# Layer 1's state-space outputs for the latents only, and one expert of full width instead of two

## What is computed

```python
for direction in range(2):
    s_ctx = diag_scan(lam_bar, einsum('blgh,gph->blgp', ug_ctx, b_bar), None, reverse)
    s_end = s_ctx[:, 0] if reverse else s_ctx[:, -1]
    s_lat = diag_scan(lam_bar, einsum('blgh,gph->blgp', ug_lat, b_bar), s_end, reverse)
    y_lat = y_lat + einsum('blgp,ghp->blgh', s_lat, cmat).real
    if need_ctx:
        y_ctx = y_ctx + einsum('blgp,ghp->blgh', s_ctx, cmat).real
```

## Time and profile before

| | us |
|---|---|
| median of 3 runs | 1811.03 (1811.0 to 1811.67) |
| profiled execution, its own time | 1811.02 |
| its span | 1809.3 |
| TensorE matmul busy | 1719.1 |
| VectorE busy | 651.3 |
| ScalarE busy | 351.9 |
| TensorE weight load busy | 909.5 |

### The profile page before, as it was taken

The page is one execution under the profiler, slowest core; times in us unless marked ns, Lnnn a source line. Parts: engine busy times, 40 slices in busy tenths (PEclk is TensorE's granted clock), DMA queues, the critical chain, the costliest instruction groups (busy, mean ns, idle before and its releaser), DMA issues.

```text
span 1809.3 us, 22168 instructions
## 1 busy us (share of the span) xinstructions
PE 1719.1 (95%) x9128; PEld 909.5 (50%) x9128; DVE 651.3 (36%) x1476; ACT 351.9 (19%) x742; POOL 73.6 (4%) x147
## 2 busy tenths in 40 slices
PE   6999999799999999988988899999999999999996
PEld 3655454288888744436766753344344322222232
DVE  5988961755554305074895520000000000000002
ACT  4324550311110000035364320000000000000001
POOL 2110100000000210000110000000000000000000
PEclk9999999899999999999999899999999999999998
DMA  8414542713333332361433089999899999999992
GB/s 304 145 20 167 188 130 81 232 48 93 94 93 79 74 78 78 111 233 47 117 91 98 1 346 370 377 375 409 318 396 359 409 347 410 392 408 344 409 377 111
DMA packets 194980, 396.11 MB, mean 219 GB/s; under 512 B 34339, under 2 KB 104587, under 8 KB 188730
## 3 DMA queue, kind: packets, MB, share of 16 engines
q1 hardware_dynamic: 189504, 391.23, 60.2%
q0 software_dynamic: 4112, 3.34, 1.2%
q10 hardware_dynamic: 1258, 0.07, 0.0%
HBM read 389.36 MB, written 1.05 MB: 216 GB/s over the span
## 4 chain that ended last, share of the span: by engine, by line
PE 87%; DVE 8%; ACT 3%; DMA 1%; issue 1%; ACTq 0%; DVEq 0%
PE ps L946 85%; PE ps L949 2%; DMA ring<-in_w_in_dram 1%; DVE rstd L1768 1%; DVE aT L1961 1%; DVE hT L1790 0%; DVE aT L1776 0%; DVE work L1785 0%; DVE aT L1785 0%; ACT work L645 0%; ACT work L646 0%; DVE work L1677 0%; DVE work L1679 0%; DVE work L1682 0%; ACT work L757 0%
## 5 line engine op out<-in xcount | busy, mean ns | idle before, releaser
L946 PE MATMUL ps<-ring,work 128*64 128x512 f32 (+4 forms) x2656 | 553.4, 515 | 1.7 <-ACT work L890 1.1
L946 PEld LDWEIGHTS ps<-ring,work 128*64 128x64 f32 (+2 forms) x2656 | 188.7, 136 | 351.9 <-issue 348.4
L946 PE MATMUL ps<-aT,ring 128*128 128x256 f32 (+1 forms) x800 | 235.4, 443 | 5.3 <-ACT work L757 2.7
L946 PE MATMUL ps<-work,ring 128*128 128x512 f32 (+1 forms) x656 | 237.0, 514 | 1.3 <-DVE work L2077 1.3
L2215 DVE TENSOR_TENSOR work<-work,ps 128x512 f32<-128x512 f32 (+4 forms) x26 | 20.1, 780 | 596.2 <-PE ps L946 596.2
L946 PE MATMUL ps<-work 128*64 128x64 f32 (+6 forms) x2016 | 205.1, 294 | 8.6 <-DVE work L2045 5.7
L946 PE MATMUL ps<-aT,work 128*128 128x256 f32 (+4 forms) x992 | 212.7, 475 | 0.0
L946 PEld LDWEIGHTS ps<-aT,ring 128*128 128x128 f32 x800 | 152.3, 192 | 75.4 <-issue 53.9
L946 PEld LDWEIGHTS ps<-work 128*64 128x64 f32 (+3 forms) x2016 | 152.9, 159 | 54.0 <-issue 40.3
L946 PEld LDWEIGHTS ps<-work,ring 128*128 128x128 f32 x656 | 124.5, 190 | 106.5 <-issue 98.5
L946 PEld LDWEIGHTS ps<-aT,work 128*128 128x128 f32 (+2 forms) x992 | 108.6, 154 | 90.5 <-issue 81.2
(11 more groups left out here) (336 smaller groups left out, 1250.7 us busy)
## 6 DMA issues: line engine op xcount, KB each, us to landing
ring<-in_moe_w_down_dram SPq DMA_DIRECT2D x70, 1024.0 KB, 8.2
ring<-in_moe_w_gate_dram SPq DMA_DIRECT2D x50, 1024.0 KB, 7.4
ring<-in_moe_w_up_dram SPq DMA_DIRECT2D x48, 1024.0 KB, 8.6
ring<-in_w_ada_dram SPq DMA_DIRECT2D x23, 2048.0 KB
ring<-in_moe_w_up_dram SPq DMA_DIRECT2D x32, 768.0 KB, 7.5
aT<-in_moe_w_down_dram SPq DMA_DIRECT2D x18, 1024.0 KB, 7.9
ring<-in_moe_w_gate_dram SPq DMA_DIRECT2D x24, 768.0 KB, 6.5
aT<-in_moe_w_up_dram SPq DMA_DIRECT2D x16, 1024.0 KB, 7.7
```

What stands on the lines that cost most here:

```text
L946: return pe.matmul(o, lhs, rhs, start=start, stop=stop)
```

## The change

Layer 1's `outputs` makes the 32 latent chunks alone, with four tiles of 32 columns side by side; U, X and Pst are laid out so that the latents' chunks lie together, the entering states are made for them alone, and the copies, the turn and the gelu behind it take half as much. Input table (1,1) of layer 1 moves ahead of `recur(1, 0)` into other tiles. ScalarE's R copies go ahead of its X copies in layer 1, and its copies of the turned tables are split from the spreading of b, which comes later; the fourth turn uses bank 0 and waits for the gelu. Of the experts only rank 0 keeps 128 slots; ranks 1 to 3 have 96, 672 in all.

```diff
--- before.py
+++ after.py
@@ -110,17 +110,18 @@
         NH = NE // 2
-        NW = NH // 2
+        NW = 1
+        NM_ = NH - NW
         TP = P // 4
-        SLOTS = [P] * NW + [HP + TP] * NW + [HP] * NH
+        SLOTS = [P] * NW + [HP + TP] * NM_ + [HP] * NH
...
-        hTs = view(7680, [2, 8, P], "b t s")
-        yH = view(9728, [D], "n")
-        yL = view(10752, [512], "n")
-        Gt = view(11264, [NE + NW, S], "r t")
+        hs = view(5376, [2, D], "b f")
+        hTs = view(7424, [2, 8, P], "b t s")
+        yH = view(9472, [D], "n")
+        yL = view(10496, [512], "n")
+        Gt = view(11008, [NE + NM_, S], "r t")
...
+        def table(l, h, qq, d):
             if qq == 0:
                 return Fq[:, d]
+            if h and l:
+                v = apad[:, :, 0, 0:S] if d == 0 else aT[:, MC:KC, 0:S]
+                return v.rearrange("p q (r x) -> p r q x", r=2)
             if h:
                 v = work[:, 13824:14848] if d == 0 else aT[:, 2:4, :].rearrange("p k t -> p (k t)")
...
-        W_BANKS = (2, 3, 4, 2)
+        W_BANKS = (2, 3, 4, 0)
         R_BANKS = (0, 1, 2, 3)
...
             def spread_in(l, h, qq, banks):
+                copy_w(l, h, qq, banks)
+                spread_b(l, h, qq)
+
+            def copy_w(l, h, qq, banks):
                 n = quarter(l, h, qq)
                 for i in range(4):
                     act.wait_ge(sem("w_turned"), 4 * n + i + 1)
                     act.activation(Wst[:, i // 2, i % 2, 4 * qq:4 * qq + 4, :],
                                    ps[:, banks[i], :].rearrange("p (q x) -> p q x", q=4), ACT.Copy).then_inc(sem("w_copied"), 1)
+
+            def spread_b(l, h, qq):
+
                 for i in range(4):
                     d, r_ = i // 2, i % 2
                     b = Bb[:, r_, d, HQ * h + 4 * qq:HQ * h + 4 * qq + 4, :].rearrange("p q (s h) -> p q s h", s=1)
-                    act.activation(table(h, qq, d)[:, r_].rearrange("p q (s h) -> p q s h", h=GH),
+                    act.activation(table(l, h, qq, d)[:, r_].rearrange("p q (s h) -> p q s h", h=GH),
                                    b.broadcast_to([P, 4, CL, GH]), ACT.Copy).then_inc(sem("b_spread"), 1)
...
+                    src = ps[0:HP, i % 4, :].rearrange("p (s b i a) -> p a s b i", s=8, i=NB, a=2)
+                    dst = dst.rearrange("p g (c i b) -> p (g c) b i", c=2, i=NB)
+                else:
+                    src = src.rearrange("p a g (b i) -> p a g b i", i=NB)
+                    dst = dst.rearrange("p g (i b) -> p g b i", i=NB)
                 act.activation(dst[0:HP], src[:, 0], ACT.Copy)
                 act.activation(dst[HP:P], src[:, 1], ACT.Copy).then_inc(sem(f"u_copied{l}"), 1)
...
-                        act.activation(o, ps[:, i, :].rearrange("p (q i b) -> p i q b", i=NB, b=NB), ACT.Copy).then_inc(sem("x_states"), 1)
+                        src = ps[:, i, :].rearrange("p (q i b) -> p i q b", i=NB, b=NB)
+                        if l:
+                            o = o.rearrange("p i q (c b) -> p i (q c) b", c=2)
+                            src = ps[:, i, :].rearrange("p (s i b) -> p i s b", s=2 * HQ, i=NB)
+                        act.activation(o, src, ACT.Copy).then_inc(sem("x_states"), 1)
                 def copy_r(h, qq, banks):
...
-                                   ps[:, b, :].rearrange("p (q t h) -> p q t h", q=4, h=GH), ACT.Copy)\
+                    n = 2 if l else 4
+                    act.activation(yt.rearrange("p t (q h) -> p q t h", h=GH)[:, n * b:n * b + n],
+                                   ps[:, b, 0:P * n].rearrange("p (q t h) -> p q t h", q=n, h=GH), ACT.Copy)\
                         .then_inc(sem("yt_copied"), 1)
                 def gelu(h):
                     act.wait_ge(sem("z_turned"), 2 * l + h + 1)
+                    if l:
+                        z = ps[0:HP, 0:2, :].rearrange("p c (t g a i b) -> p g a i b (c t)", g=2, a=2, i=NB, b=NB // 2)
+                        for a in range(2):
+                            for g in range(2):
+                                to = aT[HP * g:HP * g + HP, 2 * h + a, LAT].rearrange("p (b i t) -> p i b t", i=NB, t=CL)
+                                last = act.activation(to, z[:, g, a], ACT.Gelu_apprx_tanh)
+                            last.then_inc(sem(f"z_ready{l}"), 1)
+                        return
                     for a in range(2):
                         act.activation(aT[:, 2 * h + a, :].rearrange("p (b i t) -> p i b t", i=NB, t=CL),
...
                         copy_u(l, i)
+                    copy_r(0, 0, range(4, 8))
                     copy_x(0)
-                    copy_r(0, 0, range(4, 8))
                     vg_sig(l, 0)
                     copy_r(0, 1, range(0, 4))
...
-                spread_in(l, 1, 1, W_BANKS)
+                copy_w(l, 1, 1, W_BANKS)
                 taps(l, 0, 8, 16)
-                spread_in(l, 1, 0, W_BANKS)
+                copy_w(l, 1, 0, W_BANKS)
+                spread_b(l, 1, 1)
                 taps(l, 0, 16, 24)
                 copy_x(1)
+                spread_b(l, 1, 0)
                 taps(l, 0, 24, CW)
                 exchange(l, 2)
                 taps(l, 1, 0, 8)
...
                 act.wait_ge(sem("gates_turned"), 5 * ph + 5)
-                act.activation(Gt[:, NE:NE + NW, :].rearrange("p r (t s) -> p t r s", t=2),
-                               ps[:, 4, :].rearrange("p (t r s) -> p t r s", t=2, r=NW), ACT.Copy).then_inc(sem("moved"), 1)
+                act.activation(Gt[:, NE:NE + NM_, :].rearrange("p r (t s) -> p t r s", t=2),
+                               ps[:, 4:6, 0:P * NM_].rearrange("p t (r s) -> p t r s", r=NM_), ACT.Copy).then_inc(sem("moved"), 1)
                 def copy_turned(i):
...
-                    if banks[i] in banks[0:i]:
-                        pe.wait_ge(sem("w_copied"), 4 * n + 1 + banks.index(banks[i]))
+                    if h and i == 3:
+                        pe.wait_ge(sem(f"z_ready{l}"), 2)
                     for q in range(4):
-                        last = turn(ps[:, banks[i], P * q:P * q + P], table(h, qq, i // 2)[:, i % 2, q, :])
+                        last = turn(ps[:, banks[i], P * q:P * q + P], table(l, h, qq, i // 2)[:, i % 2, q, :])
                     last.then_inc(sem("w_turned"), 1)
...
                     pe.wait_ge(sem("p_ready"), hh + 1)
+                    rows = [slice(HP * a, HP * a + HP) for a in range(2)]
+                    if l:
+
+                        late = slice(NJ // 2, NJ)
+                        for qi in range(4):
+                            four = [(b, a, ps[TP * (2 * b + a):TP * (2 * b + a) + TP, qi // 2, P * (qi % 2):P * (qi % 2) + P])
+                                    for b in range(2) for a in range(2)]
+                            for b, a, o in four:
+                                mm(o, U[:, 2 * (HQ * h + 4 * b + qi) + a, late], K[:, b, a, qi, :], True, False)
+                            for d in range(2):
+                                lo = GH * (1 - d)
+                                for r in range(2):
+                                    for b, a, o in four:
+                                        last = mm(o, Pst[rows[a], d, r, 4 * b + qi, late], E[rows[a], d, r, 4 * b + qi, lo:lo + P],
+                                                  False, d == 1 and r == 1)
+                            if qi % 2:
+                                last.then_inc(sem("y_chunks"), 1)
+                            if qi == 1 and between:
+                                between()
+                        return
                     for b in range(2):
                         for qi in range(4):
                             q = 4 * b + qi
-                            rows = [slice(HP * a, HP * a + HP) for a in range(2)]
                             o = [ps[rows[a], b, P * qi:P * qi + P] for a in range(2)]
                             for a in range(2):
                                 mm(o[a], U[:, 2 * (HQ * h + q) + a, :], K[:, b, a, qi, :], True, False)
...
                     pe.wait_ge(sem("yt_copied"), 2 * (2 * l + h + 1))
+                    n = HP if l else P
                     for t in range(CL):
-                        last = turn(ps[:, t // 4, P * (t % 4):P * (t % 4) + P], yt[:, t, :])
+                        last = turn(ps[0:n, t // 4, P * (t % 4):P * (t % 4) + P], yt[:, t, 0:n])
                     last.then_inc(sem("z_turned"), 1)
...
                 pe.wait_ge(sem("moved"), MOVED * ph + 7)
-                for j in range(4):
-                    last = turn(ps[:, 4, P * j:P * j + P], SgB[:, j // 2, j % 2, :])
+                for i in range(2):
+                    for j in range(NM_):
+                        last = turn(ps[:, 4 + i, P * j:P * j + P], SgB[:, i, j, :])
                 last.then_inc(sem("gates_turned"), 1)
                 pe.wait_ge(sem("moved"), MOVED * (ph + 1))
...
                     if 2 * l + h:
-                        dve.wait_ge(sem("y_chunks"), 2 * (2 * l + h) - 1 + b)
```

(28 more changed lines are left out.)

23 lines of the change are left out of this document (10 added, 13 removed).

## The result

The changed kernel takes **1790.39 us** (median of 4 runs, 1789.34 to 1792.79) against 1811.35 for the kernel before beside it: a ratio of 0.9886, 95% interval 0.9869 to 0.9903. The forecast was 1786.0 with a range of 1781 to 1796, so the gain is there and the time lies in the range, 4.4 us above the forecast. The profiled execution took 1790.85 us, 20.2 less than that of the kernel before (1811.02); 24.9 were forecast. In the kernel after, helpers stand some 30 to 60 lines lower: matmuls at L978, turns at L981, the experts' product at L2277.

What follows compares the result with a forecast made beforehand. VectorE's line of tables, through the K copies, was taken to bound layer 1's mixer stretch, TensorE the experts; 16.8 (layer 1) + 0.9 (layer 0) + 6.8 + 0.4 (experts) = 24.9 us off 1811.0 gave 1786, range 1781 to 1796.

Steps and rivals of the forecast that it cites:

- Step 1: Layer 1, ScalarE's R copies before X copies: TensorE's 2.65 us stall goes, and 1.8 us of half clock behind it.
- Step 2: Layer 1, input table (1,1) moved into VectorE's idle time: saves 7.5 us in its busy line.
- Step 3: Layer 1's outputs for latents alone, four tiles side by side: 5.6 us a half in place of 11.19.
- Step 4: Layer 1's entering states halved on VectorE: saves 4.1 us in half 1, nothing in half 0.
- The new stall: Before layer 1's outputs of half 1, TensorE waits 4.4 us for K copies; 0.8 taken off for half clock.
- Step 5: Input-side copies split, bank 0 for the fourth turn: two TensorE stalls in layer 0 go, 0.9 us.
- step 6: Experts, one heavy in place of two, 672 slots for 704: 6.8 us, and 0.4 before the experts.
- The stretches forecast at nothing: Stretches expected to keep their time, with everything after the turn of half 1 keeping its durations: 0 us.
- Rival B: Half clock stays in 852.6 to 856.1 and returns behind the new stall: 1789 us, chance 0.17.
- A: Layer 1's outputs: four tiles are no faster than two; 1792 us, chance 0.10.
- C: Transfers bound the experts, pair 1 gains nothing and 9.5 us come back: 1795 us, chance 0.05.
- D: Over 96 tokens on the second expert force a second pass over the experts: about 2520 us; slower in all 0.02.

Runs made afterwards that it cites:

- experiment 4: Changed kernel with ScalarE's copies of X ahead of those of R again in layer 1: 1795.16 us, 4.8 more.
- experiment 3: Changed kernel with VectorE's input table (1,1) of layer 1 made after the gates again: 1797.35 us, 7.0 more.
- experiment 2: Changed kernel with the outputs of layer 1 given out two tiles at a time, in place of four: 1796.38 us, 6.0 more.
- Experiment 5: Changed kernel with entering states of layer 1, half 1, made for the early 32 chunks too, read by nothing: 1792.28 us, 1.9 more.
- experiment 1: Changed kernel with two 128-slot experts again (704 slots): 1796.51 us, 6.1 more.
- one piece: Changed kernel with the last K table on two queues and layer 1's outputs of half 1 unsplit by the channel sum: 1785.25 us, then 1788.94 in a second set.
- moved by 1, by 2: Changed kernel with one or two unused matmuls of 512 columns added in layer 0's feed-forward block: 1791.84 and 1792.30 us.
- moved it: Kernel before with two unused matmuls added in layer 0's feed-forward block: 1814.68 us against 1811.86 beside it.
- experiment 9: Changed kernel with the last K table's 15 copies on two queues, SP's (7) and GpSimd's (8): 1789.89 us, no difference.
- experiment 12: Kernel with two queues and half 1's outputs in one piece, plus gelu of half 1 first and sum of squares inside the GLU: 1791.07 us.

## Why the prediction was right, and what it missed

**Step 1** held in both its parts: no stall and full clock behind it, and experiment 4 brings both back (2.65 and 1.5 us).

**Step 2** held: 7.5 us forecast, 7.7 in the trace of experiment 3.

**Step 3** held: 5.6 us a half forecast, 5.52 measured; experiment 2 takes it away. With full clock the outputs of half 1 take twice 2.80.

**Step 4** held: the entering states take 5.35 us (932.58 to 937.93) for 9.49, 4.1 less, as forecast. Experiment 5 shows that they count, through the last taps and the channel sums.

**The new stall** came with half its size, 2.21 us for 4.4. The failed term is the end of the last taps, put at 2 us after the states. They end at 941.96, 4.0 us after them: ScalarE's tables pace the last three groups of four records, which start 0.85 us apart with rests of 0.20 to 0.23. It costs nothing, since the K table sets the start. The half clock that was feared there came (0.8 taken off): the first part took 4.15 for 2.80. Of these 1.35 us at most 0.5 count, since the channel sums end at 947.79 and the sum over them, which waits for them, starts at 948.25. The K copies took 12.0 us from first issue to TensorE's start, for 12.6, which gives 0.55 us of the gain.

**Step 5** is the first miss. The two stalls of layer 0 went, and TensorE was 0.92 us ahead at 347.43 (348.35 before). It kept that through a wait for VectorE and lost it behind it. TensorE, timeline, before and after:

```profile
357.02 3.75 PE L946 MATMUL ps<-work 128*128 128x256 f32 x8 [5.66 <-DVE work L2045]
...
367.76 1.89 PE L946 MATMUL ps<-work,ring 128*128 128x256 f32 x8
```

```profile
356.09 3.75 PE L978 MATMUL ps<-work 128*128 128x256 f32 x8 [5.03 <-DVE work L2107]
...
367.48 1.89 PE L978 MATMUL ps<-work,ring 128*128 128x256 f32 x8
```

It is 0.93 ahead at 356.09 and 0.28 at 367.48. In the record of the granted clock both kernels have half clock there, to 361.14 before and to 361.52 after, so the work that starts at 356.09 lies in it for 5.4 us and the work that starts at 357.02 for 4.1: 1.3 us more at half clock are 0.65 us lost. At layer 1's start 0.2 are left. The step took an earlier start for a gain and had no term for half clock further on.

**The experts (step 6)** held to 0.1 us, and ahead of them fewer slots are worth 0.8 for 0.4 (experiment 1). What the stretch shows instead, 0.5 more, is clock.

**The stretches forecast at nothing** hold the rest of the miss: 1.55 us in the projections of u, 0.4 by the new wait for the sigmoid, 1.3 ahead of pair 0 (0.5 where -0.8 was to be had), 1.7 at the end. The step that failed is the sentence that everything behind the turn keeps its durations. From the sum of squares to the product of pair 0 the same work took, against the half clock in the record of the granted clock (the stretches that begin between 990 and 1030 us):

| kernel | half clock, us | stretch, us |
|---|---|---|
| one piece, both profiles | 10.2 | 224.94, 224.93 |
| two tiles; two queues | 13.6 | 226.52, 226.41 |
| gelu first | 17.1 | 226.72 |
| early chunks too | 20.5 | 227.55 |
| after; moved by 1, by 2; table back; X first | 23.9 | 228.26; 228.27, 228.12; 228.08; 228.26 |

3.3 us of time for 13.7 us of half clock, in work that none of these edits touches. The two kernels with the old experts and mixer fit in: the kernel before took 227.77 with 17.1 us of half clock, moved it took 227.34 with 13.6, and less the 0.8 of their slots that is 227.0 and 226.6. So the 0.5 us more in this stretch are 0.8 gained and 1.3 lost to half clock. The end of the span is 29.3 us or 31.0; 31.0 came in three of the twelve profiles of kernels with the change (after, moved by one matmul, X first), each with one more stretch near 1770 us, and 29.3 in the kernel before. So 1.7 us of the 4.7 missing were most likely drawn, not made by the change. 1.55 more may be like it: the stretch near 802 us came and went between the two profiles of one kernel, but it is in nine of the twelve, and in the kernel before only when moved. What stays open is how much of the stage ahead of pair 0 is systematic: the kernel after and the five nearest to it met 23.9 us there (experiment 1 is the fifth, with the slots of before), the kernel before 17.1, or 13.6 when moved, and no experiment explains that.

**The chances.** Rival B, half clock giving back 3 us, comes nearest to what happened, at 1789, though at other places than it named. A and C are ruled out by experiments 2 and 1, D by the span, which has no room for a second pass.

## What to carry to other kernels

Add up a change against the line that ends last in its stretch, and then look for the next wait downstream that another engine sets: experiment 9 kept 0.3 of 1.4 us and experiment 12 1.0 of the 4 to 5 expected, with the channel sums and a sigmoid right behind what they hastened. An earlier start can also be lost later to half clock, as most of the 0.9 us of step 5 was. Tiles that need few columns are worth packing four abreast, here half the time for the same matmuls. Where TensorE's clock falls in stretches, times of one kernel scatter by several us between executions: judge an edit of a few us by the distance between two instructions around it, and keep 2 to 4 us for the clock in a forecast built from one trace.

## What was not expected of the hardware

- Four tiles of 64 rows by 32 columns, two row halves among them, write one PSUM bank side by side: 160 records in 5.52 us, 10.76 when given out in pairs.
- In the kernel with two queues and the outputs in one piece, GpSimd issued four copies from 932.65, paused 2.15 us before 936.89 and issued the last one at 938.45, yet TensorE waited for it until 943.59. This copy took 4.9 us from issue to landing, the last one on SP's queue in the kernel after 2.4. SP's queue had gone on to the out projection's weights from 936.77 on, while GpSimd issued its last four copies. That these held them up is likely and wasn't tried.
- Each change of ScalarE's function between root, SiLU and sigmoid costs 1.28 us of table load, and in layer 1's tail it stands on the path to the out projection.
